# Delta rule on one core: the first two tiles of each head group joined in lockstep, and waits reordered

## The chip, the cores and the metric

The kernel runs on one core of a Trainium2 chip. A core has five engines that run their own instruction streams and meet through semaphores: TensorE (PE, matrix products, with its weight loads PEld), VectorE (DVE), ScalarE (ACT), GpSimd (POOL) and SyncE (SP), which here only issues DMAs. The metric is the device time of one execution in microseconds (us). Three runs of the kernel before took 2308.81, 2309.18 and 2311.12 us; the median is 2309.18 us.

## The reference

One inference step of two layers in fp32: sparse attention and an MLP, then gated DeltaNet and an MLP. The change lies in DeltaNet's delta rule. For 16 value heads of 128 x 128 state, with chunks of 64 tokens, decays `gam` and factors `beta`:

```python
decay = jnp.where(incl, jnp.exp(jnp.where(incl, diff, 0.0)), 0.0)
a_mat = jnp.where(strict, bc[..., :, None] * jnp.einsum('...id,...jd->...ij', kc, kc) * decay, 0.0)
tinv = lax.linalg.triangular_solve(eye + a_mat, ...)       # inverse of a triangular block
value = tinv @ (vc * bc[..., None])
kcum = tinv @ (kc * (bc * jnp.exp(gam))[..., None])
...
def step(s, xs):                     # over the chunks of one sequence
    u = val - kcm @ s
    o = qd @ s + qkm @ u
    s = s * gl + jnp.swapaxes(kd, -1, -2) @ u
...
o = o * rsqrt(mean(o * o) + eps) * norm_w * silu(z)        # z = xn @ w_z
y = o @ w_out
```

There are 512 prompt tokens (one sequence) and 64 sample tokens (8 sequences of 8, each with its own state that is read and written back).

## The kernel before

`gdn_stage` (line 3211 on) is the delta rule. It takes the 16 heads as four groups `hg` of four. A group has four prompt tiles of 128 tokens (two chunks each), and then the 64 sample tokens (`seq_...`). Tiles alternate between two sets of buffers (`w.b` is 0 or 1), so that one tile can be prepared while the other is used. For each tile TensorE runs

- `first_products` (L3519 transposes of the values, L3526 the products k k and k q), `keys_turned` (L3533 transposes of the keys),
- `join`, by which the inverses of 16 x 16 blocks, computed earlier, are joined to those of 64 x 64: L3545, then VectorE, L3552 and L3556, VectorE, L3562, VectorE, L3567 and L3571, ScalarE (L3871, L3874), L3576, VectorE (L4035), L3582, ScalarE (L3879),
- the use of the tile: L3599 and L3605 (from the second tile on, products with the state), L3617 the value, L3622 the new state, L3628 the output, and later `turn` (L3639), which transposes the normed output.

ScalarE takes the exponential of the decays (`decay`, L3853), moves the values out of PSUM (`values`, L3859), scales the keys (`late_keys`, L3864), and does the steps of the join named above, the square and the root of the norm (L3887, L3892) and the output (L3897). GpSimd makes the gaps of the decays (`decay_gaps`, L3397 and L3400) out of rows that SP loads (`rows_load`, L3306), and multiplies the sample state by its decay (L3494, four instructions a group). VectorE has the steps of the join and adds the new part of the sample state (L4198).

Beside this runs z = xn @ w_z, four chunks of 128 features a group (`z_products`, L3730), eight steps of four matmuls for each chunk. It is cut into pieces that fill the gaps of the chain above: `fill(n)` issues n steps, and in groups 1 to 3 `pause(n, ...)` issues n steps of the group before, while group 0 has idle products instead (`keep_busy`, L123). A chunk collects in a pair of PSUM banks that `Z_PAIR` (L3284) names for each of the four chunks, and ScalarE empties it (`silu_z`, L3926), which counts up `z_out`. Pair 2 shares its banks with the tiles' buffers of set 1.

All orders are written out by hand: an engine runs its instructions as the Python loops emit them, and each waits for the semaphores ahead of it. On SP too, whose DMAs leave in the order of the program, a wait holds back all that stands behind it.

The feature units 12 to 15 of the convolution's output are brought to unit length late, inside `gdn_stage`, by `unit_length` (L4068 reciprocal, L4070 scale). `blocks` are the inverses of 16 x 16 blocks of the next group: keys from TensorE (`block_keys`, L3076), the substitution on GpSimd, and SP's DMAs (L3082 to L3100).

## Time and profile before

| | us |
|---|---|
| the profiled execution's own time | 2311.1 |
| its span | 2309.4 |
| three runs, median | 2309.18 |
| TensorE busy | 2182.4 |
| GpSimd busy | 1124.2 |
| VectorE busy | 1008.4 |
| ScalarE busy | 577.0 |

The profile has one execution. In a row of the timeline the first number is the start in us from the start of the span, the second the length; then come the engine, the line of the kernel, the operation with the tiles that it writes and reads, and, in brackets, how long the engine stood idle before, and whose result ended that. Consecutive instructions of the same kind are one row. Matmuls overlap a little, so that a row ends after the next one has begun. The granted clock is a share of the full clock of TensorE: 1.00 is 2.4 GHz, 0.50 is 1.2 GHz. `gdn_stage` goes from about 1243 to 1736 us; the groups begin near 1244, 1371, 1490 and 1613 us.

### The profile page before, as it was taken

What the parts mean: (1) busy time and instruction counts of PE and PEld (TensorE: products, weight loads), DVE (VectorE), ACT (ScalarE), POOL (GpSimd) and SP (SyncE); (2) the same over time, 40 slices, a digit from 0 to 9 for tenths busy, and PEclk for the clock granted to TensorE, in tenths of its full rate; (3) what the DMA queues carried; (4) which work ended last, traced back from release to release, by engine and by line L of the source; (5) the groups of instructions that cost most, each with busy time, mean ns of one, the idle gap of its engine ahead of it and who ended that gap; (6) DMA issues with size and microseconds to landing.
All of it is one profiled execution on the core that took longest, in us unless ns stands there. A gap on an engine that the chain in (4) does not pass through costs nothing. (4 is left out here: it accounts for less than half of the span.)

```text
span 2309.4 us, 33163 instructions
## 1 busy us (share of the span) xinstructions
PE 2182.4 (94%) x12590; PEld 1617.2 (70%) x12590; DVE 1008.4 (44%) x1879; ACT 577.0 (25%) x1292; POOL 1124.2 (49%) x1075
## 2 busy tenths in 40 slices
PE   9898999899999999999998898989899999999997
PEld 7675555476777777767775767676767767777776
DVE  5343676336330341357886544343443163313422
ACT  2103577501000000135554424343320010000011
POOL 3212555257654565365695243525237276644653
PEclk9999799999999999999999999999999999999999
DMA  9825001911212221432223314242303122122211
GB/s 331 223 77 184 1 2 45 327 63 66 73 59 99 80 74 73 144 90 75 68 74 73 89 42 133 54 131 56 124 24 132 73 92 73 55 76 107 73 73 41
DMA packets 125912, 216.47 MB, mean 94 GB/s; under 512 B 73602, under 2 KB 96002, under 8 KB 109762
## 3 DMA queue, kind: packets, MB, share of 16 engines
q1 hardware_dynamic: 119234, 197.13, 25.9%
q0 software_dynamic: 3088, 14.03, 1.8%
q10 hardware_dynamic: 3440, 3.25, 0.4%
q8 instruction: 102, 1.67, 0.3%
q14 instruction: 48, 0.39, 0.1%
HBM read 185.08 MB, written 37.55 MB: 96 GB/s over the span
## 5 line engine op out<-in xcount | busy, mean ns | idle before, releaser
L2014 PE MATMUL ps<-xn,ring 128*128 128x288 f32 x768 | 198.8, 407 | 5.4 <-DVE xn L2117 3.2
L2014 PE MATMUL ps<-hid,ring 128*128 128x288 f32 x768 | 192.8, 406 | 0.0
L2014 PEld LDWEIGHTS ps<-xn,ring 128*128 128x128 f32 x768 | 145.3, 190 | 48.3 <-DVE xn L2117 5.9
L2014 PEld LDWEIGHTS ps<-hid,ring 128*128 128x128 f32 x768 | 145.6, 190 | 40.7 <-ACT p L2051 0.8
L2097 POOL TENSOR_TENSOR prod<-prod,rstd 128x1152 f32<-128x1152 f32 x32 | 83.9, 2621 | 179.6 <-DVE prod L2181 163.3
L2051 ACT ACTIVATE p<-ps 128x288 f32<-128x288 f32 x48 | 19.7, 410 | 597.4 <-PE ps L2014 597.4
L3730 PE MATMUL ps<-xn,ring 128*128 128x288 f32 x512 | 149.2, 429 | 5.9 <-PE ps L3834 4.0
L1122 POOL TENSOR_SCALAR ring<-ring,fac 128x128 f32<-128x128 f32 (+2 forms) x96 | 92.2, 976 | 88.1 <-DVE fac L1551 88.1
L2014 PE MATMUL ps<-x_sum,wsum 128*128 128x288 f32 x512 | 130.5, 407 | 3.4 <-DVE x_sum L2121 1.9
L2071 POOL TENSOR_TENSOR wsum<-ring 128x512 f32<-128x512 f32 x64 | 81.9, 1279 | 99.9 <-DMA ring<-in_w_mlp 92.0
L2014 PE MATMUL ps<-hid_sum,wsum 128*128 128x288 f32 x512 | 128.4, 407 | 0.2
L3730 PEld LDWEIGHTS ps<-xn,ring 128*128 128x128 f32 x512 | 93.3, 196 | 44.6 <-issue 22.6
L2014 PEld LDWEIGHTS ps<-x_sum,wsum 128*128 128x128 f32 x512 | 96.8, 190 | 32.0 <-issue 3.2
L2014 PEld LDWEIGHTS ps<-hid_sum,wsum 128*128 128x128 f32 x512 | 96.9, 190 | 28.3 <-POOL ring L2072 1.9
L2899 DVE SCALAR_TENSOR_TENSOR x<-x,gi_convw 128x600 f32<-128x600 f32 x90 | 92.4, 1026 | 30.6 <-ACT x L2693 28.3
L2171 DVE TENSOR_TENSOR u<-p,ps 128x288 f32<-128x288 f32 x48 | 21.7, 452 | 169.1 <-PE ps L2014 169.1
L2162 DVE TENSOR_TENSOR u<-p,ps 128x288 f32<-128x288 f32 x48 | 21.8, 453 | 159.3 <-PE ps L2014 159.3
L2076 POOL TENSOR_TENSOR wsum<-ring,wsum 128x512 f32<-128x512 f32 x64 | 87.9, 1374 | 5.0
L2072 POOL TENSOR_TENSOR ring<-ring 128x512 f32<-128x512 f32 x64 | 89.1, 1392 | 0.0
L3397 POOL TENSOR_TENSOR gdn_tiles<-gdn_tiles,gdn_upto_tok 128x512 f32<-128x512 f32 x16 | 16.6, 1040 | 145.4 <-DMA gdn_tiles<-gate_rows_scratch 145.2
L2074 POOL TENSOR_TENSOR wsum<-wsum,ring 128x512 f32<-128x512 f32 x64 | 82.9, 1295 | 0.0
L1382 ACT ACTIVATE ring<-ps,nmax 128x128 f32<-128x128 f32 (+3 forms) x128 | 66.1, 523 | 58.3 <-DVE nmax L1499 58.3
(597 smaller groups left out, 4650.8 us busy)
## 6 DMA issues: line engine op xcount, KB each, us to landing
ring<-in_w_mlp SPq DMA_DIRECT2D x64, 1024.0 KB, 4.9
ring<-in_w_gdn_in SPq DMA_DIRECT2D x16, 1024.0 KB, 4.9
ring<-in_w_nsa_in SPq DMA_DIRECT2D x9, 1024.0 KB, 17.4
ring<-in_w_gdn_z SPq DMA_DIRECT2D x8, 1024.0 KB, 5.0
x<-in_seq_state SPq DMA_DIRECT2D x4, 2048.0 KB
out_seq_state<-x SPq DMA_DIRECT2D x4, 2048.0 KB, 12.1
ring<-in_w_gdn_out SPq DMA_DIRECT2D x8, 1024.0 KB, 5.6
out_win_old<-in_win_rows POOLq DMA_DIRECT2D x1, 8064.0 KB, 46.5
```

What stands on the lines that cost most here:

```text
L1122: nc.gpsimd.tensor_scalar(p, p, fac[:, job % 2, half, i:i + 1], None, ALU.mult).then_inc(scaled, 1)
L1382: nc.scalar.activation(prob[job % 3][half][:, p_at(i):p_at(i) + width(i)], S.ps[:, score_bank(k, half), 0:width(i)], ACT.Exp, bias=nmax[:, ...
L2014: mm = nc.tensor.matmul(S.ps[:, base + BANK[p], 0:HT], stationary(p, blk.units[pair // 4], pair % 4), moving(blk.kind, p, pair), start=pai ...
L2071: g.tensor_tensor(wsum[:, slot, 0], quad[:, slot, 2], quad[:, slot, 3], ALU.add).then_inc(w_summed, 1)
L2072: g.tensor_tensor(quad[:, slot, 2], quad[:, slot, 0], quad[:, slot, 2], ALU.subtract).then_inc(w_summed, 1)
L2074: g.tensor_tensor(wsum[:, slot, 1], wsum[:, slot, 0], quad[:, slot, 0], ALU.subtract).then_inc(w_summed, 1)
L2076: g.tensor_tensor(wsum[:, slot, 2], quad[:, slot, 1], wsum[:, slot, 1], ALU.subtract).then_inc(w_summed, 1)
L2097: g.tensor_tensor(prod[:, i % 2], prod[:, i % 2], S.rstd[:, 1:2, :].broadcast_to([128, 2, T]), ALU.mult).then_inc(normal, 1)
L2162: v.tensor_tensor(u2[:, n % 2], p1[:, n % 2], b, ALU.add).then_inc(u2_set, 1)
L2171: v.tensor_tensor(u3[:, n % 2], p1[:, n % 2], b, ALU.add).then_inc(u3_set, 1)
L2899: i = v.scalar_tensor_tensor(out=c_, in0=p[:, t:t + CV], scalar=tap(t), in1=c_, op0=ALU.mult, op1=ALU.add)
L3730: mm = nc.tensor.matmul(S.pairs[:, Z_PAIR[c], half, :], S.ring[:, unit % SLOTS, k * 256 + (c % 2) * 128:k * 256 + (c % 2) * 128 + 128], S. ...
```

## The change

1. The chunks of z use other pairs of banks: `Z_PAIR` (3, 3, 2, 3) becomes (3, 2, 3, 3). Chunk 1 then waits for the tiles' buffers of set 1 rather than for the silu of chunk 0, chunk 2 waits for the silu of chunk 0, and chunk 3 for that of chunk 2. `first_products` of tile 0 no longer waits for a silu, that of tile 1 for chunk 1's.
2. The joins of tiles 0 and 1 of a group run in lockstep on TensorE, VectorE and ScalarE; both tiles' first products stand ahead of them, with four steps of z's last chunk between these, and the other four on both sides of the first tile's value product. The join of tile 1 no longer lies within the use of tile 0. `block_keys` moves behind the first products of tile 2.
3. On ScalarE the exponential of a tile's decays (`decay`) moves from ahead of the previous tiles' output to behind the square; at the end of a group the exponential of the next group's tile 0 moves behind the silu of chunk 1.
4. On SP, in groups 1 to 3, the DMA of the sample state and the rows of tile 2 go ahead of the wait for z's last chunk and the load of z's weights that follows it. In the stage before, the DMAs of the block inverses (L3100) go ahead of two others.
5. On GpSimd the gaps of the next group's tile 0 move between the second and the third of the four multiplications of the sample state.
6. On VectorE unit 13's `unit_length` in group 0 moves from the start to behind the first tile's new state.

The code's core:

```diff
-        Z_PAIR = (3, 3, 2, 3)
+        Z_PAIR = (3, 2, 3, 3)
...                                                     SP
                 else:
-                    sp.wait_ge(zd.product, 4 * hg)
-                    ring_load(2 * hg + 3)
                     sp.wait_ge(seq_add, hg * 8)
                     sp.dma_start(S.out["seq_state"][hg - 1], seq_state).then_inc(seq_out, 16)
                 wait_step(sp, C[0], "pe", w[0].job, "p64")
                 rows_load(w[2])
                 t_load(w[2])
+                if hg:
+                    sp.wait_ge(zd.product, 4 * hg)
+                    ring_load(2 * hg + 3)
...                                                     POOL
                 if hg < 3:
-                    for i in (1, 0):
-                        decay_gaps(tile(hg + 1, i))
-                        grown_keys(tile(hg + 1, i))
+                    decay_gaps(tile(hg + 1, 1))
+                    grown_keys(tile(hg + 1, 1))
                 wait_step(pool, Q, "pe", hg, "value")
                 pool.wait_ge(seq_in, 16 * hg + 16)
                 for j in range(4):
+                    if j == 2 and hg < 3:
+                        decay_gaps(tile(hg + 1, 0))
+                        grown_keys(tile(hg + 1, 0))
...                                                     PE
-                    pe.wait_ge(z_out, 4 * w.hg - 1)
+                    if w.i == 1:
+                        pe.wait_ge(z_out, 4 * w.hg - 2)
...
-                            elif c == 2:
+                            elif c == 1:
                                 wait_step(pe, C[1], "vec", 2 * hg + 2)
                                 wait_step(pe, N[1], "act", 2 * hg + 2)
                             else:
-                                pe.wait_ge(z_out, 4 * hg + (1 if c == 1 else 2))
+                                pe.wait_ge(z_out, 4 * hg + (1 if c == 2 else 3))
...
                 first_products(first)
-                pause(1, 6)
+                pause(1, 2)
+                first_products(second)
+                pause(1, 4)
                 keys_turned(first)
-                pause(2, 2)
-                joins = join(first)
...
-                for _ in joins:
-                    pause(1, 1)
+                for _ in zip(join(first), join(second)):
+                    pass
                 for i in range(PT):
...
                     next(joins, None)
+                    if i == 0:
+                        pause(2, 2)
                     next(used)
                     next(joins, None)
+                    if i == 0:
+                        pause(2, 2)
...                                                     ACT
+                for f in (late_keys, joined_32, joined_64):
+                    for k in range(2):
+                        f(w[k])
...
-                    if w[i + 2]:
-                        decay(w[i + 2])
...
                     square(*norm_of(hg, i), hg, i)
                     if w[i + 2]:
+                        decay(w[i + 2])
                         values(w[i + 2])
...
                 if hg < 3:
-                    for i in (1, 0):
-                        decay(tile(hg + 1, i))
+                    decay(tile(hg + 1, 1))
                 silu_z(hg, 1)
+                if hg < 3:
+                    decay(tile(hg + 1, 0))
                 out(*norm_of(hg, PT), hg, PT)
```

How the instructions move is shown at three places; lines of the changed kernel are 4 or 5 higher than before (3734 is the old 3730, 3549 the old 3545). The first is TensorE at the start of group 1, before: the second half of tile 0's join, with z's steps (L3730), and the start of tile 1's (L3545).

```order
L3730 MATMUL ps<-xn,ring 128x288 x2
L3562 MATMUL ps<-gdn_tiles 64x64 x8
L3730 MATMUL ps<-xn,ring 128x288 x2
L3567 MATMUL ps<-gdn_tiles 64x64 x4
L3571 MATMUL ps<-gdn_tiles 64x64 x8
L3730 MATMUL ps<-xn,ring 128x288 x2
L3576 MATMUL ps<-gdn_tiles 64x64 x4
L3730 MATMUL ps<-xn,ring 128x288 x2
L3582 MATMUL ps<-gdn_tiles 64x64 x4
L3545 MATMUL ps<-gdn_tiles 64x64 x8
L3076 MATMUL ps<-gdn_qkv 32x32 x32
L3552 MATMUL ps<-gdn_tiles 64x64 x8
```

After, the same place holds both tiles' joins (L3549 to L3586), each step for both tiles, with no z between them.

```order
L3549 MATMUL ps<-gdn_tiles 64x64 x16
L3556 MATMUL ps<-gdn_tiles 64x64 x8
L3560 MATMUL ps<-gdn_tiles 64x64 x8
L3556 MATMUL ps<-gdn_tiles 64x64 x8
L3560 MATMUL ps<-gdn_tiles 64x64 x8
L3566 MATMUL ps<-gdn_tiles 64x64 x16
L3571 MATMUL ps<-gdn_tiles 64x64 x4
L3575 MATMUL ps<-gdn_tiles 64x64 x8
L3571 MATMUL ps<-gdn_tiles 64x64 x4
L3575 MATMUL ps<-gdn_tiles 64x64 x8
L3580 MATMUL ps<-gdn_tiles 64x64 x8
L3586 MATMUL ps<-gdn_tiles 64x64 x8
```

What stood between the join's steps has gone ahead of them and behind them. The second place is TensorE in the use of tile 0 of group 1, before: value (L3617), new state (L3622) and output (L3628) with tile 1's join around them, then tile 2's first products, and the first product of tile 1 with the state (L3599).

```order
L3617 MATMUL ps<-gdn_tiles 128x128 x4
L3562 MATMUL ps<-gdn_tiles 64x64 x8
L3622 MATMUL ps<-gdn_tiles 128x128 x4
L3567 MATMUL ps<-gdn_tiles 64x64 x4
L3571 MATMUL ps<-gdn_tiles 64x64 x8
L3628 MATMUL ps<-gdn_tiles 128x128 x4
L3576 MATMUL ps<-gdn_tiles 64x64 x4
L3519 MATMUL ps<-cst,gdn_qkv 128x128 x4
L3526 MATMUL ps<-gdn_qkv 128x128 x4
L3582 MATMUL ps<-gdn_tiles 64x64 x4
L3533 MATMUL ps<-cst,gdn_qkv 128x128 x2
L3599 MATMUL ps<-gdn_state,gdn_tiles 128x128 x4
```

After: z's last four steps (L3734), value (L3621), state, output, then at once tile 2's first products, the block keys, tile 2's keys (L3537), and tile 1's product with the state (L3603).

```order
L3734 MATMUL ps<-xn,ring 128x288 x4
L3621 MATMUL ps<-gdn_tiles 128x128 x4
L3734 MATMUL ps<-xn,ring 128x288 x4
L3626 MATMUL ps<-gdn_tiles 128x128 x4
L3632 MATMUL ps<-gdn_tiles 128x128 x4
L3523 MATMUL ps<-cst,gdn_qkv 128x128 x4
L3530 MATMUL ps<-gdn_qkv 128x128 x4
L3076 MATMUL ps<-gdn_qkv 32x32 x32
L3537 MATMUL ps<-cst,gdn_qkv 128x128 x2
L3603 MATMUL ps<-gdn_state,gdn_tiles 128x128 x4
```

Tile 1's join has gone from this place, and what follows the output no longer stands behind a step of it. The third place is ScalarE in group 1 from tile 0's last join step on, before: silu of z (L3926), the keys of tile 1, the table and the exponential of tile 2's decays (L3853), and behind it the join steps of tile 1 (L3871, L3874), the square and the values of tile 2.

```order
L3879 ACTIVATE gdn_tiles<-ps 64x4x64
L3926 ACTIVATE gdn_shared<-ps 128x576
L3864 ACTIVATE gdn_tiles<-ps,cst 128x128 x4
L3853 ACT_TABLE_LOAD
L3853 ACTIVATE gdn_tiles<-gdn_tiles 128x512
L3871 ACTIVATE gdn_tiles<-ps 32x4x32
L3874 ACTIVATE gdn_tiles<-ps 32x4x32 x2
L3887 ACTIVATE x<-ps 128x512
L3859 ACTIVATE gdn_tiles<-ps 128x512
L3879 ACTIVATE gdn_tiles<-ps 64x4x64
L3864 ACTIVATE gdn_tiles<-ps,cst 128x128 x4
```

After: the last join steps of both tiles (L3884), silu, the square (L3892), and only then the table and the exponential of tile 2's decays (L3858), with the values of tile 2 (L3864) behind it.

```order
L3884 ACTIVATE gdn_tiles<-ps 64x4x64 x2
L3931 ACTIVATE gdn_shared<-ps 128x576
L3892 ACTIVATE x<-ps 128x512
L3858 ACT_TABLE_LOAD
L3858 ACTIVATE gdn_tiles<-gdn_tiles 128x512
L3864 ACTIVATE gdn_tiles<-ps 128x512
L3869 ACTIVATE gdn_tiles<-ps,cst 128x128 x4
L3897 ACT_TABLE_LOAD
```

The join steps of tile 1 no longer stand behind an exponential. On SP, of the difference of the whole program, this is the start of group 1: the load of z's weights (L3319) stays as the fixed row, and the sample state and tile 2's rows and blocks (L3333, L3306, L3309) pass ahead of it.

```order
 L3312 DMA gdn_tiles<-block_inverse_scratch 128x4x128
+L3333 DMA out_seq_state<-x 128x4096
+L3306 DMA gdn_tiles<-gate_rows_scratch 128x512
+L3309 DMA gdn_tiles<-block_inverse_scratch 128x4x64
 L3319 DMA ring<-in_w_gdn_z 128x2048
-L3335 DMA out_seq_state<-x 128x4096
-L3306 DMA gdn_tiles<-gate_rows_scratch 128x512
-L3309 DMA gdn_tiles<-block_inverse_scratch 128x4x64
-L3315 DMA gdn_tiles<-gate_rows_scratch 128x512
-L3312 DMA gdn_tiles<-block_inverse_scratch 128x4x128
-L3306 DMA gdn_tiles<-gate_rows_scratch 128x512
-L3309 DMA gdn_tiles<-block_inverse_scratch 128x4x64
```

The loads of lines 3315 and 3312 for tile 2 keep their place behind the load of the weights.

## Rows read from the trace of the kernel before

**Rows 1.** The page: busy time of TensorE, its share of the span, instructions.
```profile
PE 2182.4 (94%) x12590; PEld 1617.2 (70%) x12590; DVE 1008.4 (44%) x1879; ACT 577.0 (25%) x1292; POOL 1124.2 (49%) x1075
```

**Rows 2.** Waits of TensorE: line, releaser: us in total, times, longest us.
```profile
PE ps L3576 <- ACT gdn_tiles L3871: 15.8, 3, 5.6
...
PE ps L3545 <- ACT gdn_tiles L3864: 6.2, 3, 2.1
...
PE ps L3834 <- DVE x L4198: 4.9, 3, 3.1
...
PE ps L3519 <- ACT gdn_shared L3926: 2.6, 3, 0.9
...
PE ps L3730 <- ACT gdn_shared L3926: 2.0, 4, 0.5
```

**Rows 3.** Timeline of TensorE, group 1's start: start, length, engine, line, tile, [idle <-releaser].
```profile
1474.66 1.69 PE L3834 MATMUL ps<-gdn_tiles 32*128 32x512 f32 x4 [0.89 <-DVE x L4198]
...
1490.71 0.63 PE L3519 MATMUL ps<-cst,gdn_qkv 128*128 128x128 f32 x4 [0.83 <-ACT gdn_shared L3926]
1491.18 1.06 PE L3526 MATMUL ps<-gdn_qkv 128*128 128x128 f32 x8
...
1509.47 0.68 PE L3545 MATMUL ps<-gdn_tiles 64*64 64x64 f32 x16 [2.06 <-ACT gdn_tiles L3864]
1510.08 0.80 PE L3076 MATMUL ps<-gdn_qkv 128*32 128x32 f32 x64
...
1524.20 1.11 PE L3576 MATMUL ps<-gdn_tiles 64*64 64x64 f32 x8 [5.58 <-ACT gdn_tiles L3871]
```

**Rows 4.** Stretches: length, busy time per engine, then granted clock, DMA share, GB/s.
```profile
1474.66:1480.44 5.78, 5.38 (x12) 3.02 (x12) 5.64 (x7) 0.00 (x0) 5.19 (x3) 0.70 0.98 301
1510.08:1514.44 4.36, 4.36 (x107) 4.06 (x104) 1.68 (x4) 0.59 (x1) 0.00 (x0) 0.61 0.95 355
1524.20:1527.89 3.69, 3.69 (x20) 3.44 (x20) 0.43 (x1) 1.69 (x4) 1.47 (x2) 0.52 0.27 71
```

**Rows 5.** Timeline of ScalarE, first tile of group 1.
```profile
1523.22 0.63 ACT L3853 ACTIVATE gdn_tiles<-gdn_tiles 128x512 f32<-128x512 f32 x1 [12.55 <-POOL gdn_tiles L3400]
...
1524.74 0.60 ACT L3887 ACTIVATE x<-ps 128x512 f32<-128x512 f32 x1
1526.39 0.60 ACT L3859 ACTIVATE gdn_tiles<-ps 128x512 f32<-128x512 f32 x1 [1.05 <-PE ps L3519]
```

**Rows 6.** Timeline of ScalarE, a later tile of group 0.
```profile
1412.37 1.28 ACT L3853 ACT_TABLE_LOAD   x1
1413.67 0.63 ACT L3853 ACTIVATE gdn_tiles<-gdn_tiles 128x512 f32<-128x512 f32 x1
```

**Rows 7.** Timeline of GpSimd, end of group 0 and start of group 1.
```profile
1471.88 7.97 POOL L3494 TENSOR_TENSOR x<-x,cst 128x1024 f32<-128x1024 f32 x4 [0.24 <-POOLq L3406]
1520.81 1.04 POOL L3397 TENSOR_TENSOR gdn_tiles<-gdn_tiles,gdn_upto_tok 128x512 f32<-128x512 f32 x1 [40.96 <-DMA gdn_tiles<-gate_rows_scratch]
```

**Rows 8.** Timeline of SyncE's queue, start of group 1.
```profile
1507.71 0.43 SPq L3306 DMA_DIRECT2D gdn_tiles<-gate_rows_scratch  x1
```

**Rows 9.** The DMA of line 3306: microseconds to landing.
```profile
DMA to landing us min/median/max: 3.0/4.0/13.0
```

**Rows 10.** The DMA of line 3312: microseconds to landing.
```profile
DMA to landing us min/median/max: 2.8/5.5/7.7
```

**Rows 11.** Timeline of VectorE, a join step in group 1.
```profile
1499.60 0.85 DVE L4027 TENSOR_TENSOR gdn_tiles<-gdn_tiles,ps 64x256 f32<-64x256 f32 x2
```

**Rows 12.** Timeline of VectorE, start of group 0.
```profile
1249.43 3.74 DVE L4068 RECIPROCAL rstd<-rstd 128x576 f32<-128x576 f32 x1
1253.21 1.84 DVE L4070 SCALAR_TENSOR_TENSOR gdn_qkv<-gdn_qkv,rstd 128x576 f32<-128x576 f32 x1
```

**Rows 13.** Timeline of TensorE, first two tiles of group 0.
```profile
1273.09 0.68 PE L3552 MATMUL ps<-gdn_tiles 64*64 64x64 f32 x16
...
1283.76 0.68 PE L3545 MATMUL ps<-gdn_tiles 64*64 64x64 f32 x16 [0.38 <-DVE gdn_tiles L4011]
```

More of the change, by code:

```diff
@@ L2536, in _ @@
                     conv_out(2, 4, 8, 14)
+                    sp.wait_ge(blank_out, 32)
+                    block_inverses_out(sp, blocks, place, 0)
             z.prefetched = True
             conv_out(3, 4, 6, 15)
-            sp.wait_ge(blank_out, 32)
-            block_inverses_out(sp, blocks, place, 0)
             sp.wait_ge(last_set, 32)
@@ L3355, in _ @@
                     if hg == 0:
-                        sp.wait_ge(late_unit, 2)
+                        sp.wait_ge(late_unit, LATE_ORDER.index(13) + 1)
                     else:
@@ L3471, in _ @@
                 grown_keys(tile(0, i))
-            scaled(3, KD)
+            scaled(2, KD)
             g.memset(zm, 0.0).then_inc(zm_zero, 1)
@@ L3757, in _ @@
                 first_products(first)
-                pause(1, 6)
+                pause(1, 2)
+                first_products(second)
+                pause(1, 4)
                 keys_turned(first)
-                pause(2, 2)
-                joins = join(first)
-                next(joins)
                 pause(1, 1)
-                first_products(second)
-                next(joins)
                 keys_turned(second)
                 pause(1, 1)
-                for _ in joins:
-                    pause(1, 1)
+                for _ in zip(join(first), join(second)):
+                    pass
                 for i in range(PT):
-                    used, joins, ahead = use(tile(hg, i)), (join(tile(hg, i + 1)) if i < 3 else iter(())), tile(hg, i + 2)
+                    used, joins, ahead = use(tile(hg, i)), (join(tile(hg, i + 1)) if 0 < i < 3 else iter(())), tile(hg, i + 2)
                     last = norm_before(hg, i) if i else None
@@ L3775, in _ @@
                     next(used)
-                    if i == 0 and hg < 3:
-                        pe.wait_ge(z_out, 4 * hg)
-                        if hg == 2:
-                            pe.wait_ge(late_unit, LATE)
-                        block_keys(S, hg + 1, lambda i, kh: S.ps[:, 6, 64 * i + 32 * kh:64 * i + 32 * kh + 32]).then_inc(blocks.keys_mm, 1)
                     next(joins, None)
+                    if i == 0:
+                        pause(2, 2)
                     next(used)
                     next(joins, None)
+                    if i == 0:
+                        pause(2, 2)
                     if i == 3:
@@ L3795, in _ @@
                     next(joins, None)
+                    if i == 0 and hg < 3:
+                        pe.wait_ge(z_out, 4 * hg)
+                        if hg == 2:
+                            pe.wait_ge(late_unit, LATE)
+                        block_keys(S, hg + 1, lambda i, kh: S.ps[:, 6, 64 * i + 32 * kh:64 * i + 32 * kh + 32]).then_inc(blocks.keys_mm, 1)
                     if ahead:
@@ L3922, in silu_z @@
                 if n == 0:
-                    act.wait_ge(late_unit, 3)
+                    act.wait_ge(late_unit, LATE_ORDER.index(15) + 1)
                 if hg:
@@ L3931, in _ @@
                 w = [tile(hg, i) for i in range(PT)] + [None, None]
-                if hg == 0:
-                    decay(w[0])
-                values(w[0])
-                late_keys(w[0])
-                if hg == 0:
-                    decay(w[1])
-                values(w[1])
-                joined_32(w[0])
-                joined_64(w[0])
+                for k in range(2):
+                    if hg == 0:
+                        decay(w[k])
+                    values(w[k])
+                for f in (late_keys, joined_32, joined_64):
+                    for k in range(2):
+                        f(w[k])
                 if hg:
@@ L3944, in _ @@
                     last = norm_before(hg, i) if i else None
-                    if w[i + 1]:
+                    if i and w[i + 1]:
                         late_keys(w[i + 1])
@@ L3955, in _ @@
                         out(*last, hg, i - 1)
-                    if w[i + 1]:
+                    if i and w[i + 1]:
                         joined_32(w[i + 1])
@@ L3959, in _ @@
                     if w[i + 2]:
+                        decay(w[i + 2])
                         values(w[i + 2])
-                    if w[i + 1]:
+                    if i and w[i + 1]:
                         joined_64(w[i + 1])
@@ L4129, in _ @@
                 if hg == 0:
+                    unit_inverse(12)
                     unit_length(12)
-                    unit_length(13)
                 keys(w[0])
-                joins = join(w[0])
-                next(joins)
-                next(joins)
                 keys(w[1])
-                next(joins)
-                next(joins)
+                for _ in zip(join(w[0]), join(w[1])):
+                    pass
                 for i in range(PT):
@@ L4141, in _ @@
                     norm = norm_sum(*last) if last else iter(())
-                    joins = join(w[i + 1]) if w[i + 1] else iter(())
+                    joins = join(w[i + 1]) if i and w[i + 1] else iter(())
                     next(norm, None)
@@ L4150, in _ @@
                     new_state(w[i])
+                    if (hg, i) == (0, 0):
+                        unit_inverse(13)
+                        unit_length(13)
                     next(joins, None)
@@ L4154, in _ @@
                     if (hg, i) == (0, 2):
+                        unit_inverse(15)
                         unit_length(15)
@@ L4185, in _ @@
                 if hg == 0:
+                    unit_inverse(14)
                     unit_length(14)
```

5 lines of the change are left out of this document (3 added, 2 removed).

## The prediction

> **What bounds the kernel now.** First the page: TensorE is busy 2182.4 us, 94% of the span [rows 1], so what is to be had lies in its idle time and in stretches where its clock is low. Then the waits of TensorE, kept to the lines of the changed stage [rows 2]. Five of them are touched: 15.8 us in three waits of L3576, the last join of a group's tile 1, for ScalarE's L3871; 6.2 us in three waits of L3545, the first product of that join, for ScalarE's L3864; 4.9 us of L3834 for VectorE's addition to the sample state; 2.6 us of the first products (L3519) and 2.0 us of z (L3730) for a silu. Then TensorE's timeline at the start of group 1, which shows them in place [rows 3]: 0.89, 0.83, 2.06 and 5.58 us within 50 us; groups 2 and 3 repeat it. The stretches behind these waits have a granted clock of 0.70, 0.61 and 0.52, between the two levels 0.50 and 1.00 [rows 4]. So an idle of about 2 us or more costs a second time: (1 - 0.61) x 4.36 = 1.7 us after the 2.06, (1 - 0.52) x 3.69 = 1.8 us after the 5.58, and (1 - 0.70) x 5.78 = 1.7 us after the 0.89 (which has smaller ones beside it).
>
> Why 5.58: L3871 is late since the exponential of tile 2's decays stands ahead of it on ScalarE, and that waited 12.55 us for GpSimd [rows 5]; GpSimd waited for rows [rows 7], whose DMA SP issued at 1507.71 [rows 8]. Of the landings of that line the longest is 13.0 us, the median 4.0 [rows 9]; 1507.71 + 13.0 = 1520.7, which is where GpSimd starts. The DMA leaves behind the load of z's weights and the 2 MB of sample state, as the order of SP shows.
>
> **The change part by part.** *Removed.* With the pairs of banks changed, chunk 1's wait (2.0) and that of tile 0's first products (2.6) go. The sample state: GpSimd's gaps of tile 0 stood ahead of its four multiplications of 2.0 us each [rows 7]; with the gaps behind the second, the first two are over 5 us earlier, and the two waits of 0.9 in groups 1 and 2 go with their low clock: 2 x (0.9 + 1.7) = 5.2. The longest of the three, 3.1 us, is that of group 0, where VectorE has a late unit ahead, and stays. Tile 1's join: its keys (L3864) stood behind silu and tile 0's last join step; in lockstep they come early, 6.2 + 3 x 1.7 = 11.3. L3871 of tile 1 stands before the exponential now, not behind: 15.8 + 3 x 1.8 = 21.2. Together 2.0 + 2.6 + 5.2 + 11.3 + 21.2 = 42.3 us.
>
> *What is late next: the joins themselves.* Between a tile's products VectorE has to finish its step; z filled that time. Now the other tile's products do: 16 runs of 64 x 64, 0.68 us each and some 0.57 from start to start [rows 13], 9.2 us for both tiles. VectorE's longest step is the 0.85 with 0.42 ahead of it [rows 11], against one tile's two runs of 1.1 us. That leaves from 0 to (0.85 + 0.42) = 1.3 us in a group; I take 0.5, the nearer end since the other tile covers most, in three groups 1.6.
>
> *What is late next: tile 2's keys.* After tile 0's output TensorE has first products of some 1.5 us and block keys of 0.8 [rows 3]; then `keys_turned` waits for the values, and ScalarE has the square, 0.60 [rows 5], the table, 1.28, the exponential, 0.63 [rows 6], and the values, 0.60 [rows 5], in series: 3.1 us. 3.1 - 2.2 (they overlap by 0.1), with 0.2 for two handovers, is a wait of 1.1; in group 3, without block keys, 1.9. Groups 1 to 3: 4.1. Bounds: nothing, if the table is there before the square ends; 3 x 3.1 = 9.3 if nothing covers it. The low clock behind it: 1.7 x 3 at most, 0 at least; 1.9 is near the 2.06 that brought it, 1.1 nearer the 0.83 that alone did not [rows 3, 4], so one of three: 1.6. Is the exponential ready to run then? I added up group 1 in its new order from the pieces of the old (times after the change are such sums): the joins begin near 1494.6, the rows of tile 2 leave near 1502.5, as soon as tile 0's product L3580 is out, and the load of weights and 2 MB go elsewhere in time; with the median of 4.0 they are there by 1507 and the gaps 2.5 later, ahead of the output's end at 1511.7. With 13.0 they would be there at 1515.5, and the wait 6 us longer.
>
> The exponential needs a table, and where it moved between silus the program has two table loads more at each of three boundaries. The row shows 1.28 us, and the next instruction starts 0.01 after its end [rows 6]; between silu of chunk 1 and the output ScalarE idles for several us, which hides them, and without this cover they cost 6 x 1.28 = 7.7.
>
> The Trainium skill, page "ScalarE: Activation LUTs", section "What ACT_TABLE_LOAD costs", puts a drain of about 1.38 us to the load's 1.28. The trace has no room for it between the load and the exponential [rows 6], so the measurement decides; by the page's figure the three waits for tile 2's keys would be 4 us longer and the time, as an estimate, 2280.
>
> *Other terms.* Later tiles: the exponential with its table lies now between square and values, and tile 3's values come later by 1.28 + 0.63 less what TensorE has beside it; between 0 and 1.9 in each group, I take 0.55 (the next tile's products lie beside it), four times: 2.2. In group 3 chunk 3 waits for the silu of chunk 2, an instruction like the 0.60 of [rows 5]: 0 to 1.9, taken 0.8. In group 0 unit 13, 3.74 + 1.84 us of VectorE [rows 12], no longer stands ahead of tile 0 but ahead of tile 2's keys. The start is up to 5.6 earlier, TensorE stands about 3 us before the first product of tile 2, and a low clock (1.6) comes with that; I work out 3.4 earlier at that product (1280.4 against 1283.76 [rows 13]), less 1.6: a gain of 1.8, between a loss of 2 and a gain of 5.6. SP's order in the stage before: 0.2 at most, since TensorE ends that stage later than SP; taken 0.
>
> Moved past queues: on SP, the loads of lines 3315 and 3312 for tile 2 stay behind the weights (1 MB), and these wait for z's last chunk, which now ends after tile 0's value, near 1509.6. Line 3312 leaves at about 1510.5, and with the median of 5.5 or the longest of 7.7 [rows 10] lands by 1516 to 1518.2, against a need some 3 us after tile 1's first product with the state, which comes at 1515.2 in the same sum: cost 0, with up to 2 us to spare.
>
> *The sum*: 42.3 - 1.6 - 4.1 - 1.6 - 2.2 - 0.8 + 1.8 = 33.8 us. The profiled execution took 2311.1, so it would take 2277.3; the median of the runs is 1.9 lower (2309.18), and from there it is 2275.4, say 2276.
>
> **The rivals.** *Loads land late.* Line 3312 has the weights ahead of it. If it takes the 13.0 us of the rows [rows 9], it lands at 1523.5, tile 2's join stands about 5.1 us, and the clock falls (1.7): 6.8 x 3 = 20 of the 34, leaving 2296. For: the landings of rows behind such traffic were that long. Against: 2 MB of the sample state leave some 20 us earlier now, so less is in the queues.
>
> *The clock falls in part of the lockstep.* Without z between them, the joins are 64 x 64 products alone, with small waits. If half of each such run of some 9.7 us and the stretch behind it go at half clock, that is about 6 us in four groups, 24 in all: 2300. For: idles of 0.9 with smaller ones beside them brought 0.70 [rows 4]. Against: in group 0 runs of the same kind without z keep 0.68 us, the length at the full clock [rows 13].
>
> *Slower: the clock is at 0.50 through the whole lockstep.* Then each of four groups loses 9.7 + 1.6 = 11.3 us, 45 in all, against a gain of 34: 2320. It decides from 8.5 us a group on; the place is the sixteen runs of L3549 to L3586. For it speaks only that these runs are the longest stretch without wide products in the stage; against it the same 0.68 as above.
>
> *The waits only move*: ScalarE's exponential still ends last, at the values instead of at the join, if the rows land as late as before. Then tile 2's keys wait some 6 us longer in three groups, with clock, and the rest covers the remainder: near 2300, or no change if the joins cost as well.
>
> **How the numbers follow.** A difference under 0.2%, 4.6 us, is about what a measurement of this kernel cannot tell from none. My forecast 0.68, its own range 2263 to 2288 (from the bounds of tile 2's keys and their clock, -5 to +9 together, of group 0, -4 to +4, of tile 3 and the lockstep, +-4, not all on one side). Late loads 0.11, clock in part 0.10, of which 0.03 ends within 0.2%. Slower 0.08. Waits that only move 0.03, of which 0.02 within 0.2%. So faster 0.68 + 0.11 + 0.07 + 0.01 = 0.87, same 0.05, slower 0.08. The range takes in the late loads and goes 3 us below the likeliest's own: 2260 to 2298.
>
> **What would show it.** Right: in the waits of TensorE the rows L3545 for ScalarE and L3576 for L3871 are gone (new lines 3549, 3580), the first products of a group wait for no silu, and L3537 has three waits of 1 to 2 us for ScalarE; SP's rows of tile 2 leave near the end of tile 0's join and land in some 4 us; the joins run with 0.68 us a step at clock 1.00. Wrong: a clock of 0.50 in the joins, a wait of tile 2's join for a DMA, or values that wait 5 us for GpSimd. The forecast as a whole is wrong if the five waits go and the stage, 1243 to 1736, is shorter by less than 20 us.

## The result and the profile after

The changed kernel takes 2256.81 us (median of four runs, 2255.24 to 2258.85), the kernel before beside it 2308.99 us. The ratio is 0.9774, with a 95% interval of 0.9757 to 0.979: 52.2 us less, where 33.8 were forecast. The sign and the waits came as foretold; the time lies outside the range, 3 us below its lower end, and part of what made it shorter was not in the forecast.

On the page after, with the columns of [rows 1], TensorE is busy 28.7 us less; the span is 2256.9 us, 52.5 less. It has four products fewer (12586 for 12590): group 0 now has 24 idle products in its first tiles where it had 28, some 1.8 us of work. More than half of the gain is therefore not idle time that went, but a shorter busy time of nearly the same products. That is the side which the forecast sized at 10.7 us (the low clock of [rows 4]).

```profile
PE 2153.7 (95%) x12586; PEld 1601.4 (71%) x12586; DVE 1007.5 (45%) x1879; ACT 584.6 (26%) x1298; POOL 1125.9 (50%) x1075
```

The waits of TensorE after, against [rows 2] (lines are 4 or 5 higher; 3549 is the old 3545, 3839 the old 3834):

```profile
PE ps L3549 <- DVE gdn_tiles L4014: 5.8, 8, 3.1
PE ps L3537 <- ACT gdn_tiles L3864: 5.7, 7, 1.8
...
PE ps L3621 <- DVE gdn_tiles L4047: 3.4, 1, 3.4
...
PE ps L3839 <- DVE x L4205: 2.4, 1, 2.4
...
PE ps L3571 <- DVE gdn_tiles L4034: 2.1, 4, 0.5
```

Of the five waits of before two remnants are there: one of 2.4 us of L3839 (group 0's, 3.1 before), and 1.1 us in two of z for a silu, which is not in these rows. L3537, the wait for tile 2's keys, is new, as forecast. TensorE's timeline after, which answers to [rows 3], shows both of the lockstep's prices. Counted from 0 as in the code, this is the start of group 2, and so is the place of [rows 3, 5, 7, 8, 11], from 1471 to 1528 us before; the headings of those rows, of [rows 6] and the prediction count one lower:

```profile
1475.53 1.32 PE L3566 MATMUL ps<-gdn_tiles 64*64 64x64 f32 x32
1477.39 0.62 PE L3571 MATMUL ps<-gdn_tiles 64*64 64x64 f32 x7 [0.54 <-DVE gdn_tiles L4034]
...
1489.51 0.76 PE L3076 MATMUL ps<-gdn_qkv 128*32 128x32 f32 x64
1491.36 0.44 PE L3537 MATMUL ps<-cst,gdn_qkv 128*128 128x128 f32 x2 [1.09 <-ACT gdn_tiles L3864]
```

The wait of the lockstep for VectorE is 0.54 us, the wait for the keys 1.09 (1.09 in group 1 too, and 1.8 in group 3; the rest of the 5.7 us are waits under 0.5 in later tiles). On ScalarE the chain ahead of the keys is the one that was foretold, square, table, exponential, values, and nothing on GpSimd holds it up any more [rows 5, 7]:

```profile
1486.50 0.65 ACT L3931 ACTIVATE gdn_shared<-ps 128x576 f32<-128x576 f32 x1 [4.59 <-PE ps L3734]
1488.28 0.60 ACT L3892 ACTIVATE x<-ps 128x512 f32<-128x512 f32 x1 [1.13 <-PE ps L3632]
1488.90 1.28 ACT L3858 ACT_TABLE_LOAD   x1
1490.19 0.63 ACT L3858 ACTIVATE gdn_tiles<-gdn_tiles 128x512 f32<-128x512 f32 x1
1490.73 0.58 ACT L3864 ACTIVATE gdn_tiles<-ps 128x512 f32<-128x512 f32 x1
```

SP's queue before had the weights (1 MB) and the sample state (2 MB) right ahead of the rows, which left at 1507.71 [rows 8]:

```profile
1506.84 0.35 SPq L3319 DMA_DIRECT2D ring<-in_w_gdn_z  x1
1507.23 0.43 SPq L3335 DMA_DIRECT2D out_seq_state<-x  x1
```

After, the rows leave at 1479.79, ahead of z's weights and not 0.9 us behind them; the sample state left at 1462.02.

```profile
1479.79 0.33 SPq L3306 DMA_DIRECT2D gdn_tiles<-gate_rows_scratch  x1
1480.16 0.44 SPq L3309 DMA_DIRECT2D gdn_tiles<-block_inverse_scratch  x1
1486.49 0.33 SPq L3319 DMA_DIRECT2D ring<-in_w_gdn_z  x1
```

Their landing took 13.0 us at the longest before [rows 9]; now:

```profile
DMA to landing us min/median/max: 3.0/4.1/7.3
```

Where the time went is best seen in stretches that begin with a group's first products and end with tile 1's first product with the state. Before, groups 1 to 3 (length, then busy time of TensorE, its weight loads, VectorE, ScalarE, GpSimd, the granted clock, the share of DMA, GB/s):

```profile
1371.38:1409.27 37.89, 30.15 (x371) 25.15 (x371) 10.87 (x29) 9.14 (x23) 4.78 (x4) 0.91 0.38 121
1490.71:1528.78 38.07, 30.20 (x371) 25.19 (x371) 10.87 (x29) 9.14 (x23) 4.78 (x4) 0.87 0.38 122
1610.27:1648.04 37.77, 29.67 (x306) 24.55 (x307) 10.87 (x29) 9.14 (x23) 4.78 (x4) 0.86 0.39 123
```

After, the same work:

```profile
1361.97:1388.27 26.30, 24.48 (x371) 21.54 (x370) 10.76 (x28) 10.03 (x24) 2.31 (x2) 1.00 0.31 106
1465.33:1491.63 26.30, 24.48 (x371) 21.53 (x370) 10.76 (x28) 10.03 (x24) 2.31 (x2) 1.00 0.32 109
1568.51:1594.81 26.30, 23.79 (x308) 20.88 (x306) 10.76 (x28) 10.03 (x24) 2.31 (x2) 1.00 0.31 106
```

Each became 11.5 to 11.8 us shorter, 34.8 together. Some 6 us of each is idle time; TensorE's busy time fell from 30.2 to 24.5 us (in group 3, without block keys, from 29.7 to 23.8), and the clock, 0.91 to 0.86 before, is 1.00. In steps of 1 us from 1200 us to the end of the stage, what the clock took, (1 - granted clock) x time, adds up to 27.3 us before and 6.8 after: 16 low stretches that took 1.7 us each, and 4. Of the 16, two lay mostly in idle time, in the waits for L3871 of groups 2 and 3, and took little from the products.

The diff has two things that the list of the change does not name: the four idle products, and on GpSimd two parts of xn instead of three are scaled ahead of group 0's first gaps. By the trace the second is worth 0.3 us at most, since the gaps then wait 1.09 us for their rows. The run with the joins one after the other has the 28 idle products again; the second no run takes back.

### The profile page after: what moved, and what is told of

Same layout as the page of the kernel before. It is cut to its first block and busy times, and to the rows that moved or that the text cites. A ratio compares the mean times of both kernels' runs of the same rounds, so it can differ in the third digit from the quotient of the medians.

```text
span 2256.9 us, 33164 instructions
## 1 busy us (share of the span) xinstructions
PE 2153.7 (95%) x12586; PEld 1601.4 (71%) x12586; DVE 1007.5 (45%) x1879; ACT 584.6 (26%) x1298; POOL 1125.9 (50%) x1075
## 5 line engine op out<-in xcount | busy, mean ns | idle before, releaser
L3734 PE MATMUL ps<-xn,ring 128*128 128x288 f32 x512 | 146.1, 423 | 4.4 <-PE ps L3839 3.2
L3734 PEld LDWEIGHTS ps<-xn,ring 128*128 128x128 f32 x512 | 92.1, 193 | 41.3 <-issue 20.3
L2474 POOL TENSOR_TENSOR x<-gi_prod,rstd 128x1024 f32<-128x1024 f32 (+1 forms) x16 | 36.7, 2293 | 71.5 <-DVE gi_prod L3011 67.2
```

Of the source, the lines that this page charges most:

```text
L2474: eng.tensor_tensor(p[:, first:last, 3:3 + TP], prod[:, first:last, 0:TP], S.rstd[:, 1:2, 0:TP].broadcast_to([128, m, TP]), ALU.mult).then ...
L3734: mm = nc.tensor.matmul(S.pairs[:, Z_PAIR[c], half, :], S.ring[:, unit % SLOTS, k * 256 + (c % 2) * 128:k * 256 + (c % 2) * 128 + 128], S. ...
```

## The experiments

All are variants of the changed kernel, except the lockstep alone, which is a variant of the kernel before. Times are medians; the kernel before took 2307 to 2309 us beside them.

**The joins one after the other.** Tiles 0 and 1 as before, everything else as changed.

```diff
-                for _ in zip(join(first), join(second)):
-                    pass
+                joins = join(first)
+                next(joins)
...
+                for _ in joins:
+                    pause(1, 1)
```

> The changed kernel with the joins of tiles 0 and 1 one after the other again on TensorE, VectorE and ScalarE, all other parts kept (order of SP and GpSimd, pairs of banks, the exponential behind the square). Theory A (the wait for L3871 went because the exponential was moved, not by the lockstep): TensorE waits again 2.1 us for tile 1's keys in each of groups 1 to 3, with one low stretch of 1.7 us, and some 2.5 us a group of compactness are lost, less the 1.6 us that the lockstep's own waits cost: about +5 in each of three groups and +2 in group 0, near 2274 us. Rival B (the lockstep itself took the 15.8 us away): the wait for ScalarE comes back as well, near 2295 us.

It took 2275.3 us, a ratio of 0.9867 (0.9847 to 0.9888) to before; theory A (2274). So without the lockstep some 31 of the 52 us stay. The wait for tile 1's keys is back:

```profile
PE ps L3549 <- ACT gdn_tiles L3868: 6.2, 3, 2.1
```

That for L3871 is not, so it did not need the lockstep to go. By the order on ScalarE tile 1's join steps no longer stand behind the exponential; but SP's new order is in this run as well, and it does not separate the two. The stretches of groups 1 and 2, which happened to keep the full clock:

```profile
1365.55:1395.30 29.75, 27.05 (x371) 22.18 (x370) 10.80 (x28) 9.65 (x24) 4.84 (x4) 1.00 0.31 113
1471.85:1501.61 29.76, 27.06 (x371) 22.19 (x370) 10.81 (x28) 9.66 (x24) 4.84 (x4) 1.00 0.31 113
```

So here the whole difference to the changed kernel's 26.30 us is 1.0 us more of idle time and 2.4 of work, without any clock in it. This is the term that the forecast did not have.

**The lockstep alone**, in the kernel before (SP's order, GpSimd's, ScalarE's exponential and the pairs of banks as before).

```diff
-                joins = join(first)
-                next(joins)
+                for _ in zip(join(first), join(second)):
+                    pass
```

> The kernel before with the lockstep of tiles 0 and 1 (and the places of z's steps and the block keys) alone; order of SP, GpSimd and the exponential, and the pairs of banks, as before. Theory A (without SP's order the rows still come late and the wait moves from L3576 to tile 2's keys, some 12 us in each of three groups): close to no change, 2306 us. Rival B (the lockstep by itself gives the 34.7 us that the first tiles of groups 1 to 3 gained): 2275 us.

2310.1 us, 1.0008 (0.9997 to 1.0019): no gain. The wait moved, as theory A has it, to tile 2's keys, where it is 14 us a group (12 were expected):

```profile
PE ps L3533 <- ACT gdn_tiles L3860: 42.1, 3, 14.7
```

The rows leave behind the weights as before, and their landing takes up to 14.8 us here. Before, TensorE stood 15.8 + 6.2 us for the joins. Now it stands 42.1 us for the keys, since z's steps end after tile 0's value and the DMA of the rows waits for them.

**SP's order of before** in the changed kernel.

```diff
+                    sp.wait_ge(zd.product, 4 * hg)
+                    ring_load(2 * hg + 3)
                     sp.wait_ge(seq_add, hg * 8)
...
-                if hg:
-                    sp.wait_ge(zd.product, 4 * hg)
-                    ring_load(2 * hg + 3)
```

> The changed kernel with SP's order in groups 1 to 3 as before: z's weights first, then the sample state and tile 2's rows. Theory A (the rows' 13 us were the traffic ahead of them): the rows leave 7 us later and take some 12 us to land instead of 4, so tile 2's keys wait some 12 us longer in three groups, with a low clock: about 2257 + 3 x 13.7 = 2298 us. Rival B (the landing is 4 us either way): the keys wait some 3.5 us longer, near 2268 us.

2298.7 us, 0.9965 (0.9947 to 0.9983); theory A. The wait for the keys, and the landing of the rows:

```profile
PE ps L3536 <- ACT gdn_tiles L3863: 42.3, 7, 14.1
```

```profile
DMA to landing us min/median/max: 3.0/5.0/14.5
```

Taking back SP's few lines costs 42 of the 52 us; all the rest without them is worth some 9. That is their price in the changed kernel, where z's last chunk ends later and holds back what stands behind it. The parts overlap, since 31 us stay without the lockstep, so 42 is no share of the sum. What SP's order would give alone in the kernel before was not run.

**Where z's steps stand.** Two of them between the lockstep's steps.

```diff
                 keys_turned(first)
-                pause(1, 1)
                 keys_turned(second)
-                pause(1, 1)
-                for _ in zip(join(first), join(second)):
-                    pass
+                for k, _ in enumerate(zip(join(first), join(second))):
+                    if k in (0, 2):
+                        pause(1, 1)
```

> The changed kernel with two of z's steps put between the lockstep's steps instead of ahead of them. Theory A (a run of 64 x 64 products pays some 0.1 to 0.2 us each time it changes with the wide products of z, which is why the lockstep is more compact): TensorE's work in the first tiles grows by some 0.5 us a group, its wait for VectorE of 0.5 goes: 2257 us in all, to be seen in the stretches only. Rival B (z is a better cover, changes cost nothing): 2255 us. Rival C (the joins become late for the value): 2259 us or more.

2263.1 us, 0.9802 (0.9787 to 0.9817): slower, nearest to rival C, since nothing stands any more between the keys' transposes and the joins: the joins' first products start at 1470.94 and 1471.98 in group 2, about when ScalarE has scaled tile 0's and tile 1's keys (1469.70 to 1471.88). The profile names no releaser for this wait:

```profile
PE ps L3549 <- issue: 5.7, 8, 1.1
```

But the stretches are the test of theory A, again at the full clock:

```profile
1360.13:1387.79 27.66, 25.02 (x372) 21.66 (x370) 10.76 (x29) 9.92 (x24) 2.31 (x2) 1.00 0.29 101
1464.68:1492.34 27.66, 25.02 (x372) 21.66 (x371) 10.76 (x29) 9.92 (x24) 2.31 (x2) 1.00 0.30 103
```

Counting in TensorE's timeline how often 64 x 64 products and wide ones follow each other in such a stretch gives 2 in the changed kernel, 6 here and 22 with the joins one after the other. Length less idle time is 24.67, 25.16 and 27.10 us: 0.49 / 4 = 0.12 and 2.43 / 20 = 0.12 us for each change (block keys count as wide). The same price comes from two edits, so a change between the two kinds of product costs 0.12 us here. It can be seen in single rows of this run too, where four products of z take 1.14 us among wide ones and 1.24 behind a step of the joins:

```profile
1468.31 1.14 PE L3734 MATMUL ps<-xn,ring 128*128 128x288 f32 x4
...
1472.59 1.24 PE L3734 MATMUL ps<-xn,ring 128*128 128x288 f32 x4
```

What in the change takes this time the runs do not separate.

**The gaps of both tiles first** on GpSimd, ahead of the sample state.

```diff
-                    decay_gaps(tile(hg + 1, 1))
-                    grown_keys(tile(hg + 1, 1))
+                    for i in (1, 0):
+                        decay_gaps(tile(hg + 1, i))
+                        grown_keys(tile(hg + 1, i))
```

> The changed kernel with both tiles' decay gaps on GpSimd ahead of the sample state's four multiplications, as before. Theory A: in groups 1 and 2 TensorE waits 0.9 us again for the addition to the sample state, with one low stretch of 1.7 us each, and group 0's wait grows by under 1: 2257 + 5 to 6 = 2262 us. Rival B (the addition waited for something else, chunk 1 for example): no change, 2257 us.

2266.3 us, 0.9826 (0.9802 to 0.9849). The wait is back in all three groups:

```profile
PE ps L3837 <- DVE x L4203: 6.6, 3, 3.6
```

That is 4.2 us more than in the changed kernel, and its trace has three more low stretches in these places (5.1 us). The cause is theory A's; the price, 9.5 us, is nearly twice its 5 to 6.

**The pairs of banks of before.**

```diff
-        Z_PAIR = (3, 2, 3, 3)
+        Z_PAIR = (3, 3, 2, 3)
...                                          with the waits of before
```

> The changed kernel with z's chunks on the pairs (3, 3, 2, 3) and the waits of before. Theory A: the waits of chunk 1 (2.0 us in four) and of the first products (2.6 us in three) come back, 4.6 us, without a fall of the clock: 2261.5 us. Rival B: they bring the clock down once a group, 3 x 1.7 more: 2266.5 us. Rival C: they only move to chunk 3: 2257 us.

2262.2 us, 0.9805 (0.9789 to 0.9821): 5.4 us more, theory A (4.6) within what runs differ by; no low stretch stands in groups 1 to 3, which rules out rival B. Its waits:

```profile
PE ps L3522 <- ACT gdn_shared L3930: 2.6, 3, 0.9
...
PE ps L3733 <- ACT gdn_shared L3930: 1.9, 4, 0.5
```

**Unit 13 at the start again.**

```diff
                     unit_length(12)
+                    unit_inverse(13)
+                    unit_length(13)
...
-                    if (hg, i) == (0, 0):
-                        unit_inverse(13)
-                        unit_length(13)
```

> The changed kernel with unit 13 brought to unit length ahead of tile 0's keys again. Theory A: group 0 starts 5.5 us later on VectorE, the 3.1 us wait before tile 2's join and its low stretch of 1.7 go: 2257 + 0.7 = 2258, no difference that can be told. Rival B (the move is what made group 0's 3.65 us): 2260.5 us. Rival C (TensorE's idle products hide the start): 2252 us.

2256.8 us, 0.9775 (0.976 to 0.9789), the ratio of the changed kernel: no difference, as theory A has it, but not for its reason. The wait of 3.1 us and its low stretch are gone, while TensorE does not start later: from group 0's first product to the first of the joins it is 11.70 us here (1240.46 to 1252.16) and 11.77 in the changed kernel (1242.10 to 1253.87). The idle products cover VectorE's later start, as in rival C. The 4.8 us that should come of this are not in the median, and that stays open; but unit 13's move brought TensorE no earlier start.

**The DMAs of the block inverses late again**, in the stage before.

```diff
             conv_out(3, 4, 6, 15)
+            sp.wait_ge(blank_out, 32)
+            block_inverses_out(sp, blocks, place, 0)
```

> The changed kernel with the DMAs of the block inverses in the stage before again behind the two others. Theory A (the 2.65 us by which the changed stage began earlier is a low clock at 1234 us that the change does not govern, and SP's order is worth 0.2 at most): 2257 us, no difference. Rival B (SP's order gives the start): 2259.5 us.

2261.6 us, 0.9785 (0.9768 to 0.9802); the interval overlaps that of the changed kernel (0.9757 to 0.979), so the times don't decide. The traces do. TensorE at the end of the stage before, in the kernel before:

```profile
1233.99 2.06 PE L2612 MATMUL ps<-gdn_shared,ones 128*128 128x288 f32 x4 [2.04 <-ACT gdn_shared L2715]
1235.84 6.20 PE L123 MATMUL ps<-ones 128*128 128x512 f32 x12
1244.75 1.09 PE L3519 MATMUL ps<-cst,gdn_qkv 128*128 128x128 f32 x4 [2.71 <-issue]
```

In the changed kernel:

```profile
1233.30 1.21 PE L2612 MATMUL ps<-gdn_shared,ones 128*128 128x288 f32 x4 [2.04 <-ACT gdn_shared L2715]
1234.34 5.31 PE L123 MATMUL ps<-ones 128*128 128x512 f32 x12
1242.10 0.63 PE L3523 MATMUL ps<-cst,gdn_qkv 128*128 128x128 f32 x4 [2.44 <-issue]
```

In the run with the old pairs of banks, which has the new order of SP:

```profile
1229.95 1.79 PE L2612 MATMUL ps<-gdn_shared,ones 128*128 128x288 f32 x4 [2.04 <-ACT gdn_shared L2715]
1231.54 6.47 PE L123 MATMUL ps<-ones 128*128 128x512 f32 x12
1240.45 0.89 PE L3522 MATMUL ps<-cst,gdn_qkv 128*128 128x128 f32 x4 [2.44 <-issue]
```

After the same idle of 2.04 us, the products ran at half clock in the first and third and not in the second. From that row to the changed stage's first product it is 10.8, 8.8 and 10.5 us: the low stretch is worth 1.7, SP's order 0.3. In the run with the late DMAs it is 10.8 us, with the low stretch. That low stretch is there in seven of the twelve traces of the variants: in both that have these DMAs late (this one and the lockstep alone), and in five of the ten that have them early. So the early DMAs do not prevent it; whether they make it rarer, so few traces do not show.

**Tile 2's exponential ahead of the square.**

```diff
+                    if i == 0:
+                        decay(w[2])
                     square(*norm_of(hg, i), hg, i)
                     if w[i + 2]:
-                        decay(w[i + 2])
+                        if i:
+                            decay(w[i + 2])
```

> The changed kernel with tile 2's exponential and its table ahead of tile 0's square on ScalarE (later tiles as changed). Theory A (the waits for tile 2's keys, 1.1, 1.1 and 1.8 us, are the serial chain square, table, exponential, values): they go, 2257 - 4 = 2253 us. Rival B (VectorE's keys or the gaps on GpSimd are as late): 2257 us.

2256.3 us, 0.9764 (0.9746 to 0.9783): no gain that can be told. The waits for keys went from 5.7 to 2.2 us, but a new one has come, for the block inverses' load, 1.5 us the longest:

```profile
PE ps L3537 <- ACT gdn_tiles L3864: 2.2, 5, 0.5
...
PE ps L3556 <- DMA gdn_tiles<-block_inverse_scratch: 2.0, 2, 1.5
```

It is the forecast's first rival in small: the slack of that load was about as thin as the prediction put it.

**The late units in VectorE's idle time**: 13's reciprocal behind the joins, 15's behind tile 3's norm, 14's between the sample tokens' copies.

```diff
                 for _ in zip(join(w[0]), join(w[1])):
                     pass
+                if hg == 0:
+                    unit_inverse(13)
...
+                    if (hg, i) == (0, 3):
+                        unit_inverse(15)
                     new_state(w[i])
...
+                    if (hg, j) == (0, 1):
+                        unit_inverse(14)
```

> The changed kernel with the late units 13, 15 and 14 put where VectorE idles in group 0 (unit 13's reciprocal behind the joins, unit 15's behind tile 3's norm, unit 14's between the sample tokens' copies). Theory A (TensorE's waits of 3.1, 3.4 and 2.4 us in group 0 are these units, and each brings one low stretch of 1.7 us): 2257 - 9 - 5 = 2243 us. Rival B (VectorE is late by other work in the same places): 2250 us or more.

2244.9 us, 0.9723 (0.9704 to 0.9741); theory A (2243). The waits of 3.1, 3.4 and 2.4 us are gone: L3621 and L3839 no longer wait for VectorE, L3549 waits 0.4 us at the longest, and one low stretch remains of four:

```profile
PE ps L3549 <- DVE gdn_tiles L4014: 3.1, 8, 0.4
```

**Both**, and then **z's weights behind the block inverses** as well, the lines above with, on SP,

```diff
-                if hg:
-                    sp.wait_ge(zd.product, 4 * hg)
-                    ring_load(2 * hg + 3)
...
+                inverse_load(w[2])
                 grown_load(w[2])
-                inverse_load(w[2])
+                if hg:
+                    sp.wait_ge(zd.product, 4 * hg)
+                    ring_load(2 * hg + 3)
```

> The run before with tile 2's exponential also ahead of tile 0's square. Theory A: as in the run with that edit alone, 3.5 us of waits for keys go and 2.0 us of waits for the block inverses' load come: 1.5 less than the run before, 2241 us. Rival B (no gain): 2243 us.

> The run with units and exponential moved, and on SP in groups 1 to 3 the load of z's weights behind tile 2's block inverses instead of ahead of them. Theory A (line 3312 is late since it stands behind the wait for z's last chunk and 1 MB): the 2.0 us of waits for that load go, 2239 us. Rival B (the load takes as long anyway): 2241 us.

2244.8 us, 0.9734 (0.972 to 0.9749), and 2244.8 us, 0.9732 (0.9716 to 0.9748). In the traces the waits for keys fell to 2.2 us and, in the second, those for the load went too (1.6 us in the first); the stretches of groups 1 to 3 are 1.2 us shorter each. The times don't show these 3.6 us, which is about what single runs differ by, so they decide nothing on these two edits. What is shown is the gain of the units, 12 us below the changed kernel.

## Why the prediction was right about the waits and wrong about the products' time

By TensorE's timeline, forecast and measured for each piece (us gained):

| piece | forecast | measured |
|---|---|---|
| before the stage | 0 | 2.7 |
| group 0's first tiles | 1.8 | 3.7 |
| first tiles of groups 1 to 3 | 25.2 | 34.8 |
| their later tiles | -2.2 | -0.7 |
| sample tokens of group 0 | 1.4 | 3.1 |
| sample tokens of groups 1 and 2 | 7.9 | 9.6 |
| sample tokens of group 3 | -0.3 | 0.6 |
| after the stage | 0 | -1.1 |

Right: which waits go; that the rows land late behind SP's weights and hold up the exponential (the two runs with SP's order of before have the wait at tile 2's keys); that tile 2's keys are late next, with 1.09, 1.09 and 1.8 us against 1.1, 1.1 and 1.9; the lockstep's own wait of 0.54 against 0.5, which was taken out of a span of 0 to 1.3; the clock of 1.00 in the lockstep; and that no load is late, by about 1 us. Of the rivals none came; the loads were the nearest. The idle time that was forecast to go, 33.8 - 10.7 = 23.1 us, is near the measured 52.5 - 28.7 = 23.8, in part by luck, as group 0 shows below. The miss lies in the busy time: 28.7 us against 10.7.

After too the exponential begins, at 1490.19, 0.01 us behind the end of the table's load (1488.90 + 1.28). The drain of 1.38 us that the Trainium skill, page "ScalarE: Activation LUTs", section "What ACT_TABLE_LOAD costs", adds to it is not there, and the waits for the keys came as summed without it.

Wrong is the step "what is late next: the joins themselves". It priced the lockstep by its waits alone, -1.6 us, and took the products to be as long as before. But 22 changes between small and wide products became 2, at 0.12 us each: 2.4 us a group, some 7 us in groups 1 to 3 (group 3, without block keys, had 20), of which z's own steps, 8.8 us from start to start with the joins one after the other and 8.0 in lockstep, are a third. In group 0 the full-clock work of the first tiles fell from 31.6 us (joins one after the other) to 27.2: 22 changes fewer at the same price are 2.6 of it, and the four idle products 1.8. The price of a change is shown by two edits, that of the idle products only by their length. The Trainium skill, page "TensorEngine Tiling (Array Packing)", section "Key Properties", has the rule that I had not weighed: changing the tiling mode drains TensorE. It gives no price; the runs measure 0.12 us a change, and do not show that the drain is what takes it.

The second term of the wrong size is the clock: 10.7 us were forecast, and it gave back some 16 (busy time x (1 - granted clock), in steps of 0.25 us through the stage and its approach in the two traces). Six low stretches fewer were forecast, twelve fewer came. In the first tiles of groups 1 to 3 the ones behind the removed waits cost 9.6 us of busy time (30.21, 30.26 and 29.72 against the full-clock 27.1, 27.1 and 26.4 of the joins one after the other, the last an estimate without block keys), near the 10.4 that were put down; but the one stretch in three that was expected behind tile 2's keys (1.6) did not come. In group 0 one came behind unit 13, as forecast, but one near 1258 went that was not counted. In the sample tokens of group 0 there was one more before than those counted (two at 1353 to 1361, one after), and at the stage's start 1.7 of the 2.7 us is a low stretch that comes in some traces and not in others. Some 1.5 us of busy time, in the later parts of groups 1 and 2, have no cause here.

The step on unit 13 failed too. It forecast that group 0 starts earlier on TensorE, a gain of 3.4 us less a low stretch. By the run that takes the move back the start is the same. The 3.7 us of group 0's first tiles are the changes and the idle products, 4.4 us together, less some 0.5 of waits; that the piece was forecast as a gain at all came right for another reason, by luck.

What stays open is what decides whether an idle of about 2 us is followed by a low stretch: it was in all three groups before, in one of three with the joins one after the other, and at the end of the stage before in seven of twelve variants.

## What to carry to other kernels

When a serial chain's gaps are filled with another kind of product, count the changes between the kinds, not only the waits that the filler covers: a second chain of the same kind can be the better cover. When a wait is named, follow it through every engine to the queue where it begins; here the lockstep of three engines gave nothing as long as one transfer stood late in its queue (2310.1 us), and taking that transfer's place back cost 42 us. And price a removed wait with its clock at what a row shows, but leave the count of low stretches open: here six fewer were forecast and twelve fewer came.

## What the runs showed of the hardware

A change between 64 x 64 products and wider ones costs TensorE 0.12 us in this kernel (2, 6 and 22 changes in the same work: 24.67, 25.16 and 27.10 us at a granted clock of 1.00). The low stretches of the clock in the two kernels' traces each took 1.7 us or a multiple of it, after idles from 0.9 to 5.6 us; the same idle of 2.04 us was followed by one in seven of twelve traces and not in the other five. A DMA of rows, landing in 4.0 to 5.3 us at the median, landed in 13.0, 14.5 and 14.8 us at the longest in the three runs where 3 MB were issued within 1 us ahead of it on the same queue (the kernel before, SP's order of before, the lockstep alone), and in 7.3 in the changed kernel.
